# Handing the gate and up weights to TensorE in quarters of the contraction instead of halves

## The chip, the cores and the metric

The kernel runs on one core of a Trainium2 chip. The metric is the device time of one execution in microseconds, the median of several runs. The core has a matrix engine (TensorE, PE in the profile), VectorE (DVE), ScalarE (ACT), GpSimd (POOL) and SyncE (SP), which here only starts transfers. Sixteen DMA engines move data between the main memory (HBM) and the on-chip buffer (SBUF). They are shared by all queues; nearly all transfers of this kernel are started by SP and stand in its queue, q1.

## What is computed

One step of a decoder layer on 288 tokens of width 2048 (256 of a prompt, 32 of samples), in float32: a normed input projection, a convolution mixer and a pooling mixer, an output projection, and then a mixture of experts. Each token goes to two of 32 experts:

```python
for e in range(N_EXPERTS):
    a = jax.nn.silu(hf @ w_gate[e]) * (hf @ w_up[e])
    y = y + gates[:, e:e + 1] * (a @ w_down[e])
```

w_gate[e] and w_up[e] are 2048 x 512 (4 MB each), w_down[e] is 512 x 2048 (4 MB). So an expert costs 12.6 MB of weights, whatever the number of its tokens, and the 32 of them 403 MB. A final norm follows.

## The kernel before

The mixers and the output projection fill the first 372 us. Then come the routing and the experts. Tokens are sorted into blocks of 64 slots, one block for an expert, and the experts run in pairs (function `pair`, index i, with s = 0 and 1 for the even and the odd expert, n = 2i + s). For a pair, PE first gathers the tokens of the 128 slots with one-hot matrices (`select`, L694). For an expert it then runs the gate and up product (L716): 16 steps k of the contraction (2048 = 16 x 128), each with two matmuls of 512 columns, in four groups c of four steps. The profile counts every such float32 matmul twice, so a quarter c is 16 of its records. ScalarE and VectorE make silu(gate) times up, PE transposes the result (L731) and runs the down product (L737) in four steps q. VectorE and ScalarE scale the result, and POOL scatters the rows to a table in HBM (L1359, `expert_rows`). Five more pairs exist for experts with over 64 tokens; here they are skipped by branches.

**Buffers.** Gate and up weights of an expert lie in `wgu`, 64 KB of each partition; there is one such buffer, which every expert reuses. Only the first two steps k of an odd expert have a place of their own (`wgu_first`, loaded by `load_first`, L399). In HBM, each of the 128 partitions owns 16 consecutive rows k of w_gate (32 KB), so a transfer of half the contraction takes 16384 contiguous bytes for a partition. The down weights have two buffers (`wdn[0]`, `wdn[1]`), each filled in two halves h (`load_wd`, L407), again of 16384 bytes for a partition. Before the experts start, their first pieces are loaded by `load_wd_part` (L403) with 8192 bytes for a partition.

**Order of the transfers.** SP runs one program in order. `gate_up` waits until PE has counted `gu_used` up (once per quarter c, so 4 for an expert), then starts the gate and the up transfer of a half. `down` waits for `wd_used` in the same way. In steady state the queue holds, in this order: gate and up of an odd expert (without its first two steps), down of the next even one, its gate and up, the first two steps of the next odd one, its down, and so on. The last odd expert, 31, is written out: its down weights are started after its gate and up. PE waits for a landed half on `gu_in[0]` or `gu_in[1]` (L710).

**The end.** After its last weights have landed (L484) and the scatters are done (L487), SP starts six transfers (L491) that fetch the scattered rows of the three token tiles, two for each. VectorE adds the residual to the first of each tile (L1185). PE, which has stepped over the five skipped pairs, adds up the second part and the last expert's rows in PSUM (L788, L791), VectorE adds these (L1194), and a norm and the output transfers close the program. From the second tile on, L788 waits for L1194 of the tile before (`part_added`).

Of the kernel before, what the change touches and what calls it, by code (L numbers as in the profile page):

```python
# [105 lines left out]
def hybrid_decoder_step(nc, x_prompt, x_sample, state_conv, state_pool, g_mix, w_in, w_dw, b_dw, ln_g, ln_b,  # L106
# [3 lines left out]
    with ctx:  # L110
# [3 lines left out]
        def sem(name):  # L114
            return ctx.enter_context(nc.semaphore(name))
# [107 lines left out]
        wgu = words(arena, 0, GU_WORDS).rearrange("p (c g k f) -> p c g k f", c=2, g=2, k=8)  # L223
# [35 lines left out]
        half_in = sem("half_in")  # L259
        slot_in = [sem(f"slot_in{a}") for a in range(2)]  # L260
        first_in = sem("first_in")
        gu_in = [sem(f"gu_in{c}") for c in range(2)]
        wd_in = [[sem(f"wd_in{s}{h}") for h in range(2)] for s in range(2)]

        st_out = sem("st_out")
# [35 lines left out]
        gu_used = sem("gu_used")  # L301
# [68 lines left out]
        def _(sp):  # L370
# [18 lines left out]
            sp.dma_start(wsl[0][:, 0:CT, :], wpool).then_inc(slot_in[0], 16)  # L389

            def load_gu(e, c, g, s=0):
                k = 2 if s == 1 and c == 0 else 8 * c
                w = (wgate, wup)[g][:, bass.DynSlice(e, 1), k:8 * c + 8, :].rearrange("p o k f -> p (o k f)")
                sp.dma_start(wgu[:, c, g, k - 8 * c:8, :].rearrange("p k f -> p (k f)"), w).then_inc(gu_in[c], 16)  # L394

            def load_first(e):
                for g, src in ((0, wgate), (1, wup)):
# [12 lines left out]
            for c in range(8):  # L410
                if c == 0:
                    sp.wait_ge(u_mm, CT)
                elif c == 1:
                    sp.wait_ge(wp_mm, CT)
                else:
                    sp.wait_ge(o_mm, 2 * c - 2)
                sp.dma_start(wsl[(c + 1) % 2], wout[:, :, c * COL:(c + 1) * COL]).then_inc(slot_in[(c + 1) % 2], 16)
                if c == 1:
                    sp.wait_ge(st_out, 16 * 4)
                    sp.wait_ge(old_out, 16 * 2)  # L420
                if c in (1, 3, 4, 5):
                    load_gu(0, *((0, 0), (0, 1), (1, 0), (1, 1))[(1, 3, 4, 5).index(c)])
                if c == 6:
                    sp.wait_ge(mix_ready, CT)
                    load_wd_part(0, 0, 1, 1)
                    for a in range(2):
                        sp.wait_ge(x1_ready[a], CT // 2)
                    load_wd_part(1, 1, 0, 0)
# [10 lines left out]


            def gate_up(e, n, s):
                for c in range(2):
                    sp.wait_ge(gu_used, 4 * n + 2 * c - 2)
                    for g in range(2):
                        load_gu(e, c, g, s)

# [60 lines left out]
        def _(pe):  # L507
# [190 lines left out]
            def pair(i, first=False, ahead=True, last=False):  # L698

                for s in range(2):  # L700
                    n = 2 * i + s

                    for c in range(4):
                        if first and s == 0:
                            for b in ((0, 1), (2,), (3,), ())[c]:
                                select(0, b)
                        if s == 0:
                            pe.wait_ge(xgT_ready, 4 * i + c + 1)
                        if c % 2 == 0:
                            pe.wait_ge(gu_in[c // 2], 32 * n + 32)  # L710
                        if s == 1 and c == 0:
                            pe.wait_ge(first_in, 32 * i + 32)
                        for k in range(4 * c, 4 * c + 4):
                            w = wgu_first[:, :, k, :] if s == 1 and k < 2 else wgu[:, k // 8, :, k % 8, :]
                            for h in range(2):
                                mm = pe.matmul(ps[4 + s][BLK * h:BLK * (h + 1), :], xgT[:, k, BLK * s:BLK * (s + 1)],  # L716
                                                 w[:, :, 256 * h:256 * (h + 1)], start=(k == 0), stop=(k == KT - 1))
                        mm.then_inc(gu_used, 1)
# [701 lines left out]
```

## Time and profile before

| | us |
|---|---|
| median of 3 runs | 1390.73 |
| lowest to highest | 1390.59 to 1391.2 |
| the profiled execution, its own time | 1391.43 |
| span of the profiled execution | 1389.6 |
| PE busy | 1281.5 (92%) |
| DVE, ACT, POOL busy | 344.3, 101.4, 102.4 |
| granted TensorE clock, mean | 0.974 |
| moved by DMA | 464.61 MB, mean 334 GB/s |

The span is what the trace covers from its first to its last instruction. A busy PE is not PE at its peak, since the ends of matmuls are modelled. The DMA share is the part of the time in which the 16 engines worked on packets. A share over 1 means that packets of one engine overlap.

### The profile page before, as it was taken

How to read it: one execution, taken by the hardware profiler on the slowest of the kernel's cores; microseconds unless marked ns; L12 is line 12 of the kernel's file. 1: busy time of each engine (PE TensorE's matmuls, PEld its weight loads, DVE VectorE, ACT ScalarE, POOL GpSimd, SP SyncE). 2: the span in 40 equal slices, each digit the busy share in tenths (PEclk: the TensorE clock that was granted, in tenths of full speed). 3: DMA queues.
4: the chain of work that ended last, by engine and by line, in shares of the span. 5: the costliest groups of instructions: out<-in, count | busy, mean ns of one | idle time of the engine just before them, and what ended most of it. 6: DMA issues, size and time to landing. Idle time of an engine off the chain costs nothing.

```text
span 1389.6 us, 16405 instructions
## 1 busy us (share of the span) xinstructions
PE 1281.5 (92%) x6548; PEld 721.1 (52%) x6548; DVE 344.3 (25%) x699; ACT 101.4 (7%) x232; POOL 102.4 (7%) x164
## 2 busy tenths in 40 slices
PE   9999989999999998989998989899889989889876
PEld 7777767777865443444343445444344444334321
DVE  4499933011342110101101011110101101010226
ACT  2100012000100000000000000000000000000012
POOL 2211152000000000000000000000000000000000
PEclk9999999999999999999999999999999999999997
DMA  9444325565439999999999999999999999999894
GB/s 237 165 143 158 122 67 170 199 243 211 166 138 372 426 426 427 428 430 425 428 426 426 428 427 427 427 425 428 421 427 422 418 427 419 428 426 410 341 321 118
DMA packets 82486, 464.61 MB, mean 334 GB/s; under 512 B 8079, under 2 KB 50191, under 8 KB 56195
## 3 DMA queue, kind: packets, MB, share of 16 engines
q1 hardware_dynamic: 76784, 455.89, 81.3%
q0 software_dynamic: 5392, 7.86, 1.8%
q10 hardware_dynamic: 283, 0.48, 0.1%
q8 instruction: 19, 0.31, 0.1%
q14 instruction: 8, 0.07, 0.0%
HBM read 456.67 MB, written 20.80 MB: 344 GB/s over the span
## 4 chain that ended last, share of the span: by engine, by line
PE 44%; DMA 41%; issue 7%; DVE 5%; SPq 1%; ACT 0%; DVEq 0%; ACTq 0%
DMA arena<-in_w_up_dram 41%; PE bank L716 21%; PE bank L562 14%; PE bank L737 3%; DVE arena L979 3%; PE bank L694 2%; SPq L394 1%; PE bank L788 1%; PE bank L629 1%; PE bank L646 0%; PE bank L599 0%; PE bank L511 0%; PE bank L643 0%; PE bank L791 0%; DVE arena L985 0%
## 5 line engine op out<-in xcount | busy, mean ns | idle before, releaser
L716 PE MATMUL bank<-arena,stage 128*64 128x512 f32 x1920 | 442.8, 615 | 58.3 <-DMA arena<-in_w_up_dram 58.3
L716 PEld LDWEIGHTS bank<-arena,stage 128*64 128x64 f32 x1920 | 146.0, 142 | 347.6 <-issue 304.7
L562 PE MATMUL bank<-arena,stage 128*128 128x288 f32 x1280 | 315.0, 407 | 0.8 <-DVE arena L962 0.8
L562 PEld LDWEIGHTS bank<-arena,stage 128*128 128x128 f32 x1280 | 241.9, 190 | 66.3 <-issue 0.9
L694 PEld LDWEIGHTS bank<-x1w,x1r 96*128 96x128 f32 x1536 | 174.0, 192 | 26.0 <-issue 26.0
L694 PE MATMUL bank<-x1w,x1r 96*128 96x128 f32 x1536 | 180.2, 277 | 0.0
L1222 DVE TENSOR_TENSOR a_sb<-sl_sb,bank 128x256 f32<-128x256 f32 x32 | 19.3, 604 | 498.1 <-ACT sl_sb L895 498.1
L737 PE MATMUL bank<-arena,aT 128*64 128x512 f32 x512 | 113.4, 595 | 8.5 <-ACT aT L897 8.5
L979 DVE SCALAR_TENSOR_TENSOR arena<-arena,wdw 128x256 f32<-128x256 f32 x240 | 103.0, 503 | 0.0
L1359 POOL DMA_INDIRECT expert_rows<-ysb,cur_d x31 | 30.3, 978 | 855.9 <-DVE ysb L1236 827.8
L1236 DVE TENSOR_SCALAR ysb<-bank,wslot 128x512 f32<-128x512 f32 x31 | 23.3, 751 | 255.6 <-PE bank L737 255.6
L737 PEld LDWEIGHTS bank<-arena,aT 128*64 128x64 f32 x512 | 36.4, 137 | 75.3 <-issue 73.9
L737 PE MATMUL bank<-xT,aT 128*64 128x512 f32 x256 | 58.6, 598 | 7.4 <-ACT aT L897 7.4
L737 PE MATMUL bank<-stage,aT 128*64 128x512 f32 x256 | 57.8, 592 | 0.0
L1096 DVE TENSOR_TENSOR stage<-bank,gfp 128x512 f32<-128x512 f32 x64 | 42.5, 682 | 54.2 <-PE bank L694 54.2
L895 ACT ACTIVATE sl_sb<-bank 128x256 f32<-128x256 f32 x32 | 12.3, 383 | 484.9 <-PE bank L716 484.9
L908 ACT ACTIVATE ysb<-bank,wslot 128x512 f32<-128x512 f32 x31 | 21.3, 687 | 229.6 <-PE bank L737 219.2
L737 PEld LDWEIGHTS bank<-stage,aT 128*64 128x64 f32 x256 | 18.4, 137 | 36.6 <-issue 36.6
L737 PEld LDWEIGHTS bank<-xT,aT 128*64 128x64 f32 x256 | 16.9, 136 | 38.6 <-issue 27.4
L1017 DVE TENSOR_TENSOR x1w<-bank,xT 128x288 f32<-128x288 f32 x16 | 7.2, 453 | 93.7 <-PE bank L562 93.7
L716 PE MATMUL bank<-stage 128*64 128x512 f32 x128 | 30.3, 593 | 0.0
L511 PE MATMUL bank<-ones 128*128 128x128 f32 x186 | 26.3, 309 | 1.8 <-POOL ones L1275 1.8
(232 smaller groups left out, 483.8 us busy)
## 6 DMA issues: line engine op xcount, KB each, us to landing
arena<-in_w_gate_dram SPq DMA_DIRECT2D x48, 2048.0 KB, 13.7
arena<-in_w_up_dram SPq DMA_DIRECT2D x48, 2048.0 KB, 21.1
arena<-in_w_down_dram SPq DMA_DIRECT2D x30, 2048.0 KB, 17.9
xT<-in_w_down_dram SPq DMA_DIRECT2D x15, 2048.0 KB, 20.4
stage<-in_w_down_dram SPq DMA_DIRECT2D x15, 2048.0 KB, 21.7
arena<-in_w_gate_dram SPq DMA_DIRECT2D x16, 1536.0 KB, 14.8
arena<-in_w_up_dram SPq DMA_DIRECT2D x16, 1536.0 KB, 21.1
stage<-in_w_in_dram SPq DMA_DIRECT2D x11, 2048.0 KB, 8.2
```

Of the source, the lines that this page charges most:

```text
L394: sp.dma_start(wgu[:, c, g, k - 8 * c:8, :].rearrange("p k f -> p (k f)"), w).then_inc(gu_in[c], 16)
L511: pe.matmul(ps[bank][:, 0:P], ones[:, :], ones[:, :], start=True, stop=True)
L562: last = pe.matmul(ps[bank][:, 0:NTOK], wsl[a][:, k, cc * P:(cc + 1) * P], rhs[:, k, :], start=(n == 0), stop=(n == KT - 1))
L694: last = pe.matmul(ps[SELB[b]][:, (k % 4) * P:(k % 4 + 1) * P], x1r[:, t, k * P:(k + 1) * P], hot[:, t, :], start=(t == 0), stop=(t == TT ...
L716: mm = pe.matmul(ps[4 + s][BLK * h:BLK * (h + 1), :], xgT[:, k, BLK * s:BLK * (s + 1)], w[:, :, 256 * h:256 * (h + 1)], start=(k == 0), st ...
L737: mm = pe.matmul(ps[2 + m][BLK * h:BLK * (h + 1), :], aT[:, j * P + BLK * half:j * P + BLK * (half + 1)], wdn[s][half][:, j * D + 1024 * h ...
L908: act.activation(ysb[:, s, 0:512], ps[2][:, :], ACT.Copy, scale=dyn(wslot, n, 1)).then_inc(y0_ready, 1)
L979: ins = dve.scalar_tensor_tensor(out=(fin if w == W - 1 else dst), in0=src, scalar=wdw[:, cc, w:w + 1], in1=dst, op0=ALU.mult, op1=ALU.add)
L1096: dve.tensor_tensor(xgT[:, 4 * b:4 * b + 4, :], ps[SELB[b]][:, :].rearrange("p (k s) -> p k s", k=4), gfp[:, 4 * b:4 * b + 4, None].to_bro ...
L1222: dve.tensor_tensor(a_sb[:, :].rearrange("p (j f) -> p f j", j=2), sl_sb[:, :].rearrange("p (f j) -> p f j", j=2), ps[4 + s][:, 256:512].r ...
L1236: dve.tensor_scalar(ysb[:, s, 512:1024], ps[3][:, :], dyn(wslot, n, 1), None, ALU.mult).then_inc(y1_ready, 1)
L1359: pool.indirect_dma_start(out=yexp_dram, out_offset=bass.IndirectOffsetOnAxis(ap=at, axis=0), in_=rows, in_offset=None, bounds_check=4 * N ...
```

## The change

The gate and up weights of an expert are moved and released in quarters of the contraction. `load_gu` takes c from 0 to 3 and moves four steps k (8192 contiguous bytes for a partition) instead of eight; for an odd expert, c = 0 moves the two steps that `wgu_first` doesn't hold. `gu_in` has four semaphores, and PE waits for one ahead of every quarter. SP waits for `gu_used` ahead of each quarter, and for quarter c only until PE is done with the same quarter of the expert before: 4n + c - 3 in place of 4n - 2 and 4n for the two halves. An expert has eight such transfers instead of four. The first expert's weights, loaded during the output projection, are started in four places as before, now as gate and up of one quarter together rather than as one half of one matrix. Layout, bytes and arithmetic are the same.

```diff
@@ -259,7 +259,7 @@
         half_in = sem("half_in")
         slot_in = [sem(f"slot_in{a}") for a in range(2)]
         first_in = sem("first_in")
-        gu_in = [sem(f"gu_in{c}") for c in range(2)]
+        gu_in = [sem(f"gu_in{c}") for c in range(4)]
         wd_in = [[sem(f"wd_in{s}{h}") for h in range(2)] for s in range(2)]
 
         st_out = sem("st_out")
@@ -389,9 +389,10 @@
             sp.dma_start(wsl[0][:, 0:CT, :], wpool).then_inc(slot_in[0], 16)
 
             def load_gu(e, c, g, s=0):
-                k = 2 if s == 1 and c == 0 else 8 * c
-                w = (wgate, wup)[g][:, bass.DynSlice(e, 1), k:8 * c + 8, :].rearrange("p o k f -> p (o k f)")
-                sp.dma_start(wgu[:, c, g, k - 8 * c:8, :].rearrange("p k f -> p (k f)"), w).then_inc(gu_in[c], 16)
+                k0, k1 = (2 if s == 1 and c == 0 else 4 * c), 4 * c + 4
+                o = 8 * (c // 2)
+                w = (wgate, wup)[g][:, bass.DynSlice(e, 1), k0:k1, :].rearrange("p o k f -> p (o k f)")
+                sp.dma_start(wgu[:, c // 2, g, k0 - o:k1 - o, :].rearrange("p k f -> p (k f)"), w).then_inc(gu_in[c], 16)
 
             def load_first(e):
                 for g, src in ((0, wgate), (1, wup)):
@@ -419,7 +420,8 @@
                     sp.wait_ge(st_out, 16 * 4)
                     sp.wait_ge(old_out, 16 * 2)
                 if c in (1, 3, 4, 5):
-                    load_gu(0, *((0, 0), (0, 1), (1, 0), (1, 1))[(1, 3, 4, 5).index(c)])
+                    for g in range(2):
+                        load_gu(0, (1, 3, 4, 5).index(c), g)
                 if c == 6:
                     sp.wait_ge(mix_ready, CT)
                     load_wd_part(0, 0, 1, 1)
@@ -439,8 +441,8 @@
 
 
             def gate_up(e, n, s):
-                for c in range(2):
-                    sp.wait_ge(gu_used, 4 * n + 2 * c - 2)
+                for c in range(4):
+                    sp.wait_ge(gu_used, 4 * n + c - 3)
                     for g in range(2):
                         load_gu(e, c, g, s)
 
@@ -706,8 +708,7 @@
                                 select(0, b)
                         if s == 0:
                             pe.wait_ge(xgT_ready, 4 * i + c + 1)
-                        if c % 2 == 0:
-                            pe.wait_ge(gu_in[c // 2], 32 * n + 32)
+                        pe.wait_ge(gu_in[c], 32 * n + 32)
                         if s == 1 and c == 0:
                             pe.wait_ge(first_in, 32 * i + 32)
                         for k in range(4 * c, 4 * c + 4):
```

On SP, in the loop over pairs, this is the gate and up load of an even expert before (`wgu` lies in `arena`; 4096 elements are 16384 bytes):

```order
53 L394 DMA arena<-in_w_gate_dram 128x4096 [waits gu_used]
54 L394 DMA arena<-in_w_up_dram 128x4096
55 L394 ISA [waits gu_used]
56 L394 DMA arena<-in_w_gate_dram 128x4096
57 L394 DMA arena<-in_w_up_dram 128x4096
```

And the same place now (2048 elements are 8192 bytes; `L445` and `ISA` rows work out the number to wait for):

```order
65 L395 DMA arena<-in_w_gate_dram 128x2048 [waits gu_used]
66 L395 DMA arena<-in_w_up_dram 128x2048
67 L445 REGISTER_ALU
68 L395 ISA [waits gu_used]
69 L395 DMA arena<-in_w_gate_dram 128x2048
70 L395 DMA arena<-in_w_up_dram 128x2048
71 L445 REGISTER_ALU
72 L395 ISA [waits gu_used]
73 L395 DMA arena<-in_w_gate_dram 128x2048
74 L395 DMA arena<-in_w_up_dram 128x2048
75 L395 ISA [waits gu_used]
76 L395 DMA arena<-in_w_gate_dram 128x2048
77 L395 DMA arena<-in_w_up_dram 128x2048
```

Two waits and four transfers have become four waits and eight transfers.

On PE, in the loop, this is the gate and up product of the odd expert before (the first four matmuls read `wgu_first`, which lies in `stage`):

```order
211 L716 MATMUL bank<-stage 64x512 [waits first_in]
212 L716 MATMUL bank<-stage 64x512 x3
213 L716 MATMUL bank<-arena,stage 64x512 x12
214 L716 MATMUL bank<-arena,stage 64x512 [waits gu_in1]
215 L716 MATMUL bank<-arena,stage 64x512 x15
```

And now:

```order
215 L717 MATMUL bank<-stage 64x512 [waits first_in]
216 L717 MATMUL bank<-stage 64x512 x3
217 L717 MATMUL bank<-arena,stage 64x512 x4
218 L717 MATMUL bank<-arena,stage 64x512 [waits gu_in1]
219 L717 MATMUL bank<-arena,stage 64x512 x7
220 L717 MATMUL bank<-arena,stage 64x512 [waits gu_in2]
221 L717 MATMUL bank<-arena,stage 64x512 x7
222 L717 MATMUL bank<-arena,stage 64x512 [waits gu_in3]
223 L717 MATMUL bank<-arena,stage 64x512 x7
```

The one wait in the middle of the 32 matmuls has become three, one ahead of each further quarter; no matmul has moved.

## Rows read from the trace of the kernel before

**Rows 1.** The page: DMA share (tenths) and rate in 40 slices of the span.
```profile
DMA  9444325565439999999999999999999999999894
GB/s 237 165 143 158 122 67 170 199 243 211 166 138 372 426 426 427 428 430 425 428 426 426 428 427 427 427 425 428 421 427 422 418 427 419 428 426 410 341 321 118
```

**Rows 2.** Chain of waits, 560 to 640 us: start, duration, what the end hung on.
```profile
577.90 13.76 PE bank L716 x64
...
592.23 22.64 DMA arena<-in_w_up_dram
...
614.91 8.81 PE bank L716 x32
```

**Rows 3.** DMA queues in the saturated stretch, 540 to 1240 us: packets, MB, share.
```profile
DMA packets 26850, 297.99 MB, mean 426 GB/s; under 512 B 5104, under 2 KB 5104, under 8 KB 8891
...
q1 hardware_dynamic: 23538, 294.61, 99.4%
q0 software_dynamic: 3312, 3.39, 1.4%
```

**Rows 4.** DMA queue, 378 to 384.9 us: first halves of the down weights, 8192-byte rows.
```profile
DMA packets 407, 2.95 MB, mean 427 GB/s; under 512 B 47, under 2 KB 47, under 8 KB 47
...
q1 hardware_dynamic: 407, 2.95, 101.3%
```

**Rows 5.** DMA queue, 419 to 427 us: gate and up rows of 16384 bytes.
```profile
DMA packets 224, 3.41 MB, mean 426 GB/s; under 512 B 16, under 2 KB 16, under 8 KB 16
...
q1 hardware_dynamic: 224, 3.41, 99.6%
```

**Rows 6.** Timeline of SP and PE at the start of the expert stage.
```profile
396.83 3.65 PE L716 MATMUL bank<-arena,stage 128*64 128x512 f32 x16
...
407.13 0.34 SPq L394 DMA_DIRECT2D arena<-in_w_gate_dram  x1
...
432.90 1.94 PE L716 MATMUL bank<-stage 128*64 128x512 f32 x8
434.66 12.19 PE L716 MATMUL bank<-arena,stage 128*64 128x512 f32 x56
...
440.02 0.33 SPq L394 DMA_DIRECT2D arena<-in_w_gate_dram  x1
```

**Rows 7.** Windows: PE, PEld, DVE, ACT, POOL busy, clock, DMA share, GB/s.
```profile
440.00:441.00 1.00, 1.00 (x6) 0.29 (x4) 0.00 (x0) 0.00 (x0) 0.00 (x0) 1.00 0.39 119
...
1300.00:1305.00 5.00, 4.17 (x20) 1.15 (x16) 0.24 (x1) 0.00 (x0) 0.31 (x2) 1.00 0.48 197
...
1314.00:1315.00 1.00, 1.00 (x8) 0.49 (x6) 0.00 (x0) 0.00 (x0) 0.00 (x0) 1.00 0.14 61
1315.00:1316.00 1.00, 1.00 (x7) 0.19 (x3) 0.00 (x0) 0.02 (x1) 0.00 (x0) 1.00 0.17 74
```

**Rows 8.** Timeline of PE and SP, last two experts.
```profile
1304.21 0.33 SPq L394 DMA_DIRECT2D arena<-in_w_gate_dram  x1
...
1307.10 8.78 PE L716 MATMUL bank<-arena,stage 128*64 128x512 f32 x32 [2.93 <-DMA arena<-in_w_up_dram]
...
1315.91 0.33 SPq L394 DMA_DIRECT2D arena<-in_w_gate_dram  x1
...
1317.95 7.09 PE L737 MATMUL bank<-arena,aT 128*64 128x512 f32 x32 [0.46 <-ACT aT L897]
...
1326.58 12.19 PE L716 MATMUL bank<-arena,stage 128*64 128x512 f32 x56
...
1338.38 3.12 SPq L491 DMA_DIRECT2D arena<-expert_rows  x6
```

**Rows 9.** Timeline of DVE and PE in the last stage.
```profile
1358.21 3.68 DVE L1185 TENSOR_TENSOR arena<-arena,x1r 96x2048 f32<-96x2048 f32 x1 [3.19 <-DMA arena<-expert_rows]
1361.81 1.27 DVE L1194 TENSOR_TENSOR arena<-arena,bank 96x512 f32<-96x512 f32 x2
...
1364.89 1.96 PE L788 MATMUL bank<-arena,ident 96*96 96x512 f32 x4
```

## The prediction, made before the changed kernel ran

> **What bounds the kernel now.** I read the page's slices first. From slice 14, 450 us on, to slice 36 the DMA engines are full and move 420 to 430 GB/s; before that they have room [rows 1]. Such a stretch ends when its bytes are through. The chain of waits says the same from PE's side: PE does a half of the contraction, SP starts the next transfers, they land 22.64 us later, PE does the next half in 7 to 9 us and so on [rows 2]. A 2 MB transfer at 427 GB/s takes 4.9 us, so 22 us to landing is a queue of several transfers, not latency. PE has some 3 us to spare for an expert: it sat idle 2.93 us ahead of a half [rows 8]. So an earlier release or a finer wait can't speed up the middle. It counts only where the engines run dry, at the start and at the end; and whatever makes a byte dearer counts for all experts.
>
> **The price of smaller pieces.** Per expert and engine, 32 packets of 16384 bytes (or 12288) become 64 smaller ones, and four more transfers bring four more end packets of 4 bytes. The down weights at 378 us are already read in 8192-byte rows. There 407 packets, 360 of them of 8192 bytes and 47 ends, took 101.3% of 16 x 6.9 us, that is 111.8 us, or 0.621 us for two large ones with their ends [rows 4]. At 419 us, 208 packets of 16384 bytes and 16 ends took 99.6% of 16 x 8 us, 127.5 us, or 0.613 us each [rows 5]. The difference, 0.0084 us, times 32 is **0.27 us for an expert**. That is the dear end, since packets of one engine overlap: in the full stretch the shares of the two queues add up to 100.8%, and 0.8% of 16 x 700 us over 26850 packets is 3.3 ns for each [rows 3]. 36 new packets overlap their neighbours too, 0.12 us. I take **0.15 us**. The cheap end is nothing: the rates of the two stretches, 427 and 426 GB/s, don't differ [rows 4, 5]. Between the ends I stay with 0.15, as it is made of durations and their overlap, while the rates also hold the stretches' edges. Experts 2 to 31 come through the full queue: 30 x 0.15 = **+4.5 us** on the last landing, with 0 and 30 x 0.27 = 8.1 as ends.
>
> A rule speaks against the change here. The full queue shows no time between transfers: q1 alone is 99.4% busy with fourteen transfers for a pair of experts [rows 3]. The Trainium skill, page "DMA: Bandwidth & Descriptors", section "Anatomy of one DMA", gives a fit of a fixed 2.0 us for every transfer plus its bytes at 436 GB/s (for GpSimd's path), and "Rules for kernel authors" asks for at least 1 MiB per transfer for full bandwidth; the changed ones are just 1 MiB. If the 2 us stood in the stream, eight more transfers for a pair would make it 16 us longer, 240 us in all by that page; the trace doesn't agree that it does, since it is latency at the end of each transfer, behind which the next already moves.
>
> **Start of the expert stage.** Expert 2's first transfers wait for half of expert 1, which PE began at 432.90, and are started at 440.02. With the new wait, one quarter is enough: 432.90 + 3.6 = 436.5, with a quarter at 3.65 us [rows 6]. Before, the queue ran out: in 440 to 441 the engines were busy 0.39 of the time [rows 7], until the packets of 440.02 arrived some 1.2 us later. After, the new ones stand in the queue before it is empty. What counts is how long the engine that finished last was idle, not the mean over the engines. The last landing of an expert waits for the slowest, and some engines lag: in 1300 to 1305, with nothing started before 1304.21, 0.48 of them still worked [rows 7, 8]. I take **-0.7 us**, between 0.3 and the 1.4 us or so that the mean engine was idle. The releases before (407.13 comes forward by a quarter and a gather) fill room which the engines have anyway, since the stream is held up again by the down weights of expert 2, whose wait doesn't change.
>
> **End, transfers.** Expert 31's second half waits for all of expert 30 and starts at 1315.91. The queue had nearly run dry: 0.14 and 0.17 in the two microseconds before [rows 7, 8]. After, quarters 2 and 3 wait for quarters 2 and 3 of expert 30, and quarter 2 is queued before the first two are through. For the slowest engine this is **-0.6 us** (0 to 1.1). Sum for the landing of the last down weights, which now lets SP start L491 at 1338.38 [rows 8]: 4.5 - 0.7 - 0.6 = **+3.2 us**.
>
> **End, PE.** Expert 30's second half lands at about 1307.0, and PE then needs 8.78 us for 32 records before it goes on [rows 8]. After, only the last quarter is left, 3.65 us at full clock: the quarter before it landed 4.9 us earlier. That is **-5.1 us** (3.4 if PE runs at the lower clock again). The landing itself is 29 x 0.15 - 0.7 = 3.65 us later. PE's own chain through the down product of expert 30 (1317.95) and all of expert 31 [rows 8] so ends 3.65 - 5.1 = **-1.5 us**, earlier than before. Expert 31's last quarter (7 MB of gate and up and 1 MB of the first two steps, 19.6 us after the stream passes expert 30) is there before PE needs it, at some 23 us (3.65, then 2.05 to the down product, 7.09, and three quarters); its down weights are there within a microsecond of PE's need.
>
> **Which of the two ends last.** SP starts the six transfers of L491 only when the last down weights have landed. VectorE's third residual add waits for its rows until 1358.21; L1194 follows it at 1361.81, to 1363.08. PE's L788 for the second tile needs that and started at 1364.89, held by PE's own order [rows 9]. So the transfers have **1.8 us** of slack ahead of PE. The landing is 3.2 us late and PE is 1.5 us early, so the new last comer is the row transfers with VectorE's adds: the end moves by 3.2 - 1.8 = **+1.4 us**. From there the sequence of L788, L791, L1194 and the norm is unchanged.
>
> **Edits with one answer.** The extra waits of PE are in its own order and cost nothing while it has 3 us to spare for an expert. SP's four more starts for an expert, 0.33 us each, lie in its waits. Behind SP's new waits stand the down weights of the next expert; their turn in the queue comes over 10 us later, so nobody waits for that. Expert 0's weights are started in the output projection, where the engines have room [rows 1], and are long there. Should PE's spare time be gone, a wait would cost what it lasts; it would have to grow by 3 us for an expert first.
>
> **The rivals.**
> (a) The split costs its dear end. For: durations of packets are measured directly, the overlap is a mean. Against: 0.8% of overlap must be somewhere. Then the landing moves by 8.1 - 1.3 = +6.8 and the end by +5.0: **1395.7 us**, slower. It decides from 0.20 us for an expert, where 30 x 0.20 - 1.3 - 1.8 reaches 2.9 us. It ends on the other side.
> (b) The split costs nothing. For: equal rates [rows 4, 5]. Then the landing is 1.3 us early, PE is 0.7 + 5.1 = 5.8 us early, and the end is held by VectorE's first two L1194, 1.3 us earlier than 1363.08, against 1364.89: 3.1 us sooner, **1387.6 us**, faster.
> (c) Each start of a transfer leaves a hole. At 0.1 us for each of 120 new transfers, +12 us: about **1401 us**, slower. Against: fourteen transfers for a pair leave no visible hole in 700 us [rows 3]. This is the page's rule in a mild form.
>
> **How the numbers follow.** The sum is made on the profiled execution (span 1389.6, own time 1391.43), which lies 0.7 us above the median, so the change is added to the median 1390.73: **1392.1 us**. About 0.2%, 2.8 us, is what a measurement can tell from none. The forecast with its variants (0.03 to 0.19 us for an expert) has 0.52, (a) 0.27, (b) 0.15, (c) 0.06. So: within 0.2% 0.52, slower 0.33, faster 0.15. The range leaves out most of (c), the dear tail of (a) and the cheapest of (b): 1388.0 to 1397.0. The forecast's own range is 1389 to 1393.5.
>
> **What the changed profile would show.** The step on price: the time from one landing of the last gate and up transfer to the next, over many experts, grows by 0.15 us from about 30 (12.7 MB with the scatter at 426 GB/s [rows 3]); 0.27 or 0 would speak for (a) or (b). Packets of about 0.310 us for 8192 bytes, the DMA share still 1.01 and no dip between transfers; a dip speaks for (c). The step on the start: no slice under 0.9 between 436 and 442 us. The step on the end: 16 records of L717 after the last wait of expert 30 instead of 32, the down product of expert 31 ending 1 to 2 us before 1348, while SP starts the row transfers near 1341.5 instead of 1338.38, and VectorE's last residual add starts near 1361.4. The forecast is wrong if rows in the middle are dearer than at 378 us, where few other packets ran, if the slow engines' lag changes, or if the row transfers themselves take another time at their new place.

## The result, and the profile after

The changed kernel took 1402.89 us in the median of 20 runs (1393.76 to 1409.87), the kernel before 1390.38 us in 20 (1388.87 to 1392.86). The ratio is 1.0084, 95% interval 1.0061 to 1.0108: slower, and above the whole range that was forecast (1388 to 1397). The middle of its ten faster runs, 1395.0, would lie inside that range. The spread is as telling as the median. The 20 times of before lie within 4 us. Those of the changed kernel fall into two groups: ten from 1393.76 to 1398.83 us (middle 1395.0) and ten from 1406.96 to 1409.87 us (middle 1408.3), with nothing between. So there are two things to explain: +4.6 us in the lower group, and 13 us more in the upper one.

The profile of one execution of the lower group (1394.51 us). Page: busy time, DMA share and rate in 40 slices, and the gate and up product (busy, mean ns, idle before it):

```profile
span 1392.7 us, 16789 instructions
...
PE 1266.9 (91%) x6548; PEld 713.5 (51%) x6548; DVE 343.8 (25%) x699; ACT 101.5 (7%) x232; POOL 102.4 (7%) x164
...
DMA  9444325565449999999999999999999999999974
GB/s 239 163 148 153 121 71 168 200 245 204 174 182 367 421 423 425 423 423 422 423 423 424 422 423 422 422 423 424 422 423 422 422 421 423 421 422 420 372 270 128
...
L717 PE MATMUL bank<-arena,stage 128*64 128x512 f32 x1920 | 429.4, 595 | 74.4 <-DMA arena<-in_w_up_dram 74.4
```

Against [rows 1] most of the full slices move 422 to 424 GB/s instead of 425 to 428. The DMA engines are as full as before, with more packets for the same bytes. From 540 to 1240 us:

```profile
DMA packets 40074, 295.87 MB, mean 423 GB/s; under 512 B 6573, under 2 KB 6573, under 8 KB 13132
...
q1 hardware_dynamic: 36762, 292.48, 99.9%
q0 software_dynamic: 3312, 3.39, 1.4%
```

40074 packets for 295.87 MB, where [rows 3] had 26850 for 297.99 MB; the shares of the queues add up to 101.3% instead of 100.8%. So the packets overlap more in sum, as assumed, but their durations have grown by more than that gives back. For the 12.58 MB of an expert, q1's packets took 0.994 x 700 us / 294.61 MB x 12.58 MB = 29.71 us of every engine before, and 0.999 x 700 / 292.48 x 12.58 = 30.08 us now: +0.37 us.

How much this costs an expert is best read from the chain of waits, from landing to landing of the last gate and up transfer of an expert. The kernel before (start, duration, what it was):

```profile
531.85 22.66 DMA arena<-in_w_up_dram
...
1284.39 22.57 DMA arena<-in_w_up_dram
```

The changed kernel:

```profile
527.25 26.27 DMA arena<-in_w_up_dram
553.57 3.68 PE bank L717 x16
557.82 26.00 DMA arena<-in_w_up_dram
583.95 3.67 PE bank L717 x16
...
1287.07 26.14 DMA arena<-in_w_up_dram
1313.35 3.67 PE bank L717 x16
```

Before: 554.51 to 1306.96 us for 25 experts, **30.10 us** each. After: 553.52 to 1313.21, **30.39 us**. The transfers now need 26 us instead of 22.6 from start to landing (they are started a quarter earlier), and PE does 16 records after the last one, 3.68 us, where [rows 2] had 32 in 7 to 9 us. None of that shortens the period.

The end of the same execution: timelines of PE, then of SP, then of VectorE.

```profile
1308.42 3.65 PE L717 MATMUL bank<-arena,stage 128*64 128x512 f32 x16 [1.56 <-DMA arena<-in_w_up_dram]
1313.35 3.65 PE L717 MATMUL bank<-arena,stage 128*64 128x512 f32 x16 [1.28 <-DMA arena<-in_w_up_dram]
...
1347.12 1.89 PE L738 MATMUL bank<-stage,aT 128*64 128x512 f32 x8
1356.27 3.70 PE L789 MATMUL bank<-arena,ident 96*96 96x512 f32 x4 [7.27 <-issue]
...
1368.01 1.93 PE L789 MATMUL bank<-arena,ident 96*96 96x512 f32 x4 [2.61 <-DVE arena L1195]
...
1343.55 3.94 SPq L493 DMA_DIRECT2D arena<-expert_rows  x6
...
1362.98 3.69 DVE L1186 TENSOR_TENSOR arena<-arena,x1r 96x2048 f32<-96x2048 f32 x1 [2.77 <-DMA arena<-expert_rows]
1366.58 2.47 DVE L1195 TENSOR_TENSOR arena<-arena,bank 96x512 f32<-96x512 f32 x4
```

This is the end that was forecast, step by step. PE's last wait for expert 30 is followed by 16 records instead of the 32 of [rows 8]. SP starts the row transfers at 1343.55 instead of 1338.38. VectorE's third residual add starts at 1362.98 instead of 1358.21 [rows 9], and PE, which had come last before, now stands 2.61 us in front of L789 (L788 before) for VectorE's L1195. It starts the second tile at 1368.01 instead of 1364.89, +3.1 us, and that is the whole difference of the two spans (1392.7 and 1389.6).

### The profile page after: what moved, and what is told of

It reads as the page before. It is cut to its first block, busy times and chain, and to the rows that moved or that the text cites. A ratio compares the mean times of both kernels' runs of the same rounds, so it can differ in the third digit from the quotient of the medians.

```text
span 1392.7 us, 16789 instructions
## 1 busy us (share of the span) xinstructions
PE 1266.9 (91%) x6548; PEld 713.5 (51%) x6548; DVE 343.8 (25%) x699; ACT 101.5 (7%) x232; POOL 102.4 (7%) x164
## 4 chain that ended last, share of the span: by engine, by line
DMA 52%; PE 33%; issue 7%; DVE 5%; SPq 1%; ACT 0%; DVEq 0%; ACTq 0%
DMA arena<-in_w_up_dram 49%; PE bank L564 13%; PE bank L717 12%; DVE arena L980 3%; PE bank L696 2%; PE bank L738 2%; DMA stage<-in_w_down_dram 2%; DMA arena<-expert_rows 1%; SPq L395 1%; PE bank L631 1%; PE bank L648 0%; PE bank L601 0%; PE bank L645 0%; DVE arena L986 0%; DVE arena L1195 0%
## 5 line engine op out<-in xcount | busy, mean ns | idle before, releaser
L717 PE MATMUL bank<-arena,stage 128*64 128x512 f32 x1920 | 429.4, 595 | 74.4 <-DMA arena<-in_w_up_dram 74.4
L717 PEld LDWEIGHTS bank<-arena,stage 128*64 128x64 f32 x1920 | 139.4, 137 | 356.9 <-issue 293.4
L1360 POOL DMA_INDIRECT expert_rows<-ysb,cur_d x31 | 30.3, 978 | 858.6 <-DVE ysb L1237 832.1
L717 PE MATMUL bank<-stage 128*64 128x512 f32 x128 | 30.3, 593 | 0.0
```

The lines of the kernel that those rows point to most:

```text
L1360: pool.indirect_dma_start(out=yexp_dram, out_offset=bass.IndirectOffsetOnAxis(ap=at, axis=0), in_=rows, in_offset=None, bounds_check=4 * N ...
```

## The experiments

Each ran beside the kernel before on the same chip. A time is the median of its runs; "group" means the two groups above. Half of the changed kernel's runs are of the upper one, so five runs that show none of it would come by chance once in 32.

**1. The changed kernel again**, without an edit.

> The changed kernel once more, for more times and a second trace. Its 20 times fall in two groups, 1394 to 1399 us and 1407 to 1410 us, while the trace with 1394.5 us shows 30.39 us from landing to landing of the last gate and up transfer of successive experts (before: 30.10). Theory P (packets and transfer ends make the stream dearer, and on some runs on one DMA engine more than on the others): in a run of the slow group the period is about 30.8 us, the middle takes all of the additional 13 us and the end looks the same. Rival E (something at the start or the end goes one of two ways, such as a transfer that misses its turn): the period stays 30.39 in both groups, and the 13 us show in one place.

Six times: 1398.13 twice, and 1406.75 to 1409.28 four times. The profiled one is of the upper group (1409.28 us). Its last landing, and its end (SP, then PE):

```profile
1289.07 26.18 DMA arena<-in_w_up_dram
```

```profile
1345.61 3.37 SPq L493 DMA_DIRECT2D arena<-expert_rows  x6
...
1349.14 1.89 PE L738 MATMUL bank<-stage,aT 128*64 128x512 f32 x8
1373.49 3.70 PE L789 MATMUL bank<-arena,ident 96*96 96x512 f32 x4 [22.46 <-issue]
```

The last landing is at 1315.25, the period over 25 experts (from 555.39) 30.39 us, as in the other trace. The landing is 2.0 us later than in the other trace, and the row transfers and PE with it. The rest of the difference of 14.8 us between the two spans stands in one row: PE ended its last down product at 1351.0 and then stood **22.46 us** before the first L789, where the lower group's trace has 7.27: 15.2 us more, less the 2.6 us of standing for VectorE that fall away. "issue" says that it waited for nothing the profile shows. In between it steps over the five skipped pairs, each a jump over a large piece of program. What else differs there is PE's code. Queue q8 carries instructions, 16 KB a packet; the profile doesn't name the engine, and that it is PE's is read from when its packets come. The two views, 1335 to 1375 us, of the lower group's trace and of this one:

```profile
q8 instruction: 3, 0.05, 0.6%
```

```profile
q8 instruction: 5, 0.08, 1.1%
```

Three packets of code against five. So rival E of this run held: the middle is the same in both groups.

**2. Split in halves.** The transfers of the changed kernel, the waits of before.

```diff
-                k = 2 if s == 1 and c == 0 else 8 * c
-                w = (wgate, wup)[g][:, bass.DynSlice(e, 1), k:8 * c + 8, :].rearrange("p o k f -> p (o k f)")
-                sp.dma_start(wgu[:, c, g, k - 8 * c:8, :].rearrange("p k f -> p (k f)"), w).then_inc(gu_in[c], 16)
+                for a, b in ((2 if s == 1 and c == 0 else 0, 4), (4, 8)):
+                    w = (wgate, wup)[g][:, bass.DynSlice(e, 1), 8 * c + a:8 * c + b, :].rearrange("p o k f -> p (o k f)")
+                    sp.dma_start(wgu[:, c, g, a:b, :].rearrange("p k f -> p (k f)"), w).then_inc(gu_in[c], 16)
...
-                            pe.wait_ge(gu_in[c // 2], 32 * n + 32)
+                            pe.wait_ge(gu_in[c // 2], 64 * n + 64)
```

> Eight transfers of 8192 bytes for a partition as in the changed kernel, but released and waited for in halves as before. Theory P: as dear in the middle as the changed kernel (30.4 us or more for an expert), and without the gains at the start and at the end: 1397 to 1400 us in the faster group, 1410 to 1414 in the slower, if it has one. Rival H (the finer hand-over itself disturbs the stream, by transfers started at other moments): 30.1 us for an expert and the time of the kernel before, about 1391 us.

1399.71 us (1397.69 to 1401.07), ratio 1.0064 (1.0051 to 1.0077), one group. Period 30.39 us, last landing of expert 30 at 1315.91. The whole dearer stream is there without the finer hand-over; what the hand-over gives is missing (some 4.7 us against the lower group), and so is the upper group. Theory P's first half held.

**3. Pieces of 8192 bytes in transfers of 2 MB.** The buffer is laid out by quarters (c=4, k=4), and a half of a matrix is one transfer with two pieces for each partition. The cut shows the main lines; the first half of an odd expert is left out, two transfers for each matrix.

```diff
+                    sp.dma_start(wgu[:, 2 * c:2 * c + 2, g, :, :].rearrange("p b k f -> p b (k f)"),
+                                 src.rearrange("p o (b k) f -> p (o b) (k f)", b=2)).then_inc(gu_in[c], 16)
```

> Four transfers of 2 MB for an expert as before, in halves, but the buffer is laid out by quarters, so that each partition's row is written in two pieces of 8192 bytes (an odd expert's first half is two transfers for each matrix). The number of pieces is that of the changed kernel, the number of transfers nearly that of before. If the pieces cost (32 more for an expert and DMA engine, at about 5 ns): 30.3 us for an expert, 1395 to 1398 us. If the transfers cost (their starts or their ends): near 1391 to 1392 us.

1400.62 us (1399.68 to 1402.09), ratio 1.0070 (1.0057 to 1.0083); period 30.38 us, where 30.3 us and 1395 to 1398 us were expected: at 5 ns for a piece the price was put too low. The pieces cost, not the number of transfers: this kernel has ten of them for a pair of experts instead of sixteen and pays the same.

**4. Pieces of 4096 bytes**, four transfers for an expert. The cut leaves out the buffer's layout.

```diff
+                w = (wgate, wup)[g][:, bass.DynSlice(e, 1), k:8 * c + 8, :].rearrange("p o (b k) f -> p (o b) (k f)", k=2)
+                sp.dma_start(wgu[:, 4 * c + (k - 8 * c) // 2:4 * c + 4, g, :, :].rearrange("p b k f -> p b (k f)"), w).then_inc(gu_in[c], 16)
```

> Four transfers for an expert in halves, each partition's row written in pieces of 4096 bytes: 128 pieces for an expert and DMA engine instead of 32. The pieces of 8192 bytes cost 0.29 us for an expert by the landings (30.39 against 30.10 us), that is 9 ns for each of the 32 additional ones. If each piece costs the same: 96 additional ones, +0.87 us, 30.97 us for an expert, and 1417 to 1419 us. If the price comes from something of 8192 bytes only, or from the layout, 30.4 us and 1400.

1412.27 us (1411.78 to 1415.48), ratio 1.0159 (1.0144 to 1.0173). From the chain, the first and the last landing:

```profile
537.56 19.91 DMA arena<-in_w_up_dram
...
1306.54 23.19 DMA arena<-in_w_up_dram
```

557.47 to 1329.73 us is 30.89 us for an expert, +0.79. The 96 additional pieces of the expectation hold for an even expert only; an odd one had pieces of 4096 and 12288 bytes before and gets 80. Between the two landings q1 has 60692 packets, and 25287 in the kernel before between its own two, which makes 88 more for an expert and DMA engine. That is 9.0 ns for each, next to 8.7 ns for each of 32 in rows_8k (+0.28) and 9 ns in the changed kernel (+0.29, with four more transfer ends). The price goes with the number of pieces. The whole time came out 5 us under the 1417 expected, 2 of them by the pieces that aren't there.

**5. Eight transfers over half the partitions**, with pieces of 16384 bytes.

```diff
+                for p0 in (0, 64):
+                    w = (wgate, wup)[g][p0:p0 + 64, bass.DynSlice(e, 1), k:8 * c + 8, :].rearrange("p o k f -> p (o k f)")
+                    sp.dma_start(wgu[p0:p0 + 64, c, g, k - 8 * c:8, :].rearrange("p k f -> p (k f)"), w).then_inc(gu_in[c], 16)
```

> Eight transfers for an expert of 1 MB, each with 64 partitions and rows of 16384 bytes (12288 for an odd expert's first half), in halves. The number of transfers is that of the changed kernel, the pieces are those of before. If the transfers cost: as much as the changed kernel without its gains, 1396 us or more, with two groups if these come from transfers. If the pieces cost: 1391 to 1392 us, one group.

2137.76 us (1970.56 to 2165.64). It was meant to count transfers and instead showed something else. DMA queues, 600 to 1200 us:

```profile
DMA packets 13540, 143.47 MB, mean 239 GB/s; under 512 B 3110, under 2 KB 3110, under 8 KB 4830
...
q1 hardware_dynamic: 11956, 141.66, 93.8%
```

The engines were 93.8% busy and moved 239 GB/s: for the same bytes, q1's packets took 1.7 times as long, on the mean over this stretch (0.938 x 600 us for 141.66 MB, against [rows 3]). All six runs show it; why is open. It can't tell transfers from pieces; experiment 3 did.

**6. PE's extra waits alone.** The kernel before, with PE waiting ahead of every quarter for the landed half.

```diff
-                        if c % 2 == 0:
-                            pe.wait_ge(gu_in[c // 2], 32 * n + 32)
+                        pe.wait_ge(gu_in[c // 2], 32 * n + 32)
```

> The kernel before; only PE waits ahead of every quarter, twice for the same landed half, so that its program has the rows of the changed kernel while no transfer changes. In the trace of the slower group (1409.28 us) PE stood still for 22.5 us between the last down product and the first L789, while it stepped over the five skipped pairs, against 7.3 us in the trace of 1394.5 us and 7.9 in the kernel before. Theory C (it is PE's own program: the waits have changed where its code is fetched): two groups, 1391 and about 1405 us. Rival T (it is the moment at which PE comes there, or what the transfers do then): one group at 1390 to 1392 us.

1390.65 us (1389.32 to 1392.87), 11 runs, ratio 0.9996 (0.9987 to 1.0005), one group. The waits are free, and PE's longer program alone does not make the upper group.

**7. and 8. One branch around the skipped pairs**, in the changed kernel and in the one before.

```diff
+            with pe.If(n_over > 0):
-            with pe.Fori(0, OVP) as j:
+                with pe.Fori(0, OVP) as j:
```

> The changed kernel with one more branch on PE, around the loop over the five skipped pairs, so that PE jumps once instead of five times. If the stepping over is the slower group's 13 us: one group at about 1394 to 1395 us (the faster group keeps its time, since VectorE and the row transfers end last there, not PE). If the slower group has another cause, two groups stay.

> The kernel before with the same one branch. There PE ends last (L788 of the second tile started 1.8 us after VectorE had made it possible). If the 7.9 us of stepping over shrink to some 2 us, the end moves to VectorE's order, 1.8 us sooner: 1388.6 us. If jumping once costs as much, 1390.5.

The changed kernel with it: 1399.40 us (1397.12 to 1400.44), one group, ratio 1.0057 (1.0044 to 1.0070). The upper group is gone, but the time is not that of the lower one, 1394 to 1395, that was expected. PE came to the first L790 (L788 before) 3 us sooner, had to stand for VectorE longer, 4.98 us, and ran the next matmuls at half its clock:

```profile
1353.47 3.70 PE L790 MATMUL bank<-arena,ident 96*96 96x512 f32 x4 [3.98 <-DMA arena<-expert_rows]
...
1367.61 3.70 PE L790 MATMUL bank<-arena,ident 96*96 96x512 f32 x4 [4.98 <-DVE arena L1196]
```

3.70 us where the changed kernel had 1.93 for the same four; with the four behind them the trace loses 2.7 us by that. The kernel before with one branch: 1389.53 us (1385.44 to 1392.15, 12 runs), ratio 0.9989 (0.9980 to 0.9999), some 1.2 us better: the only version here whose interval lies below 1, and only just. PE stands 4.03 us, where the kernel before had 7.91, and VectorE ends last:

```profile
1352.93 3.70 PE L789 MATMUL bank<-arena,ident 96*96 96x512 f32 x4 [4.03 <-issue]
...
1364.05 1.93 PE L789 MATMUL bank<-arena,ident 96*96 96x512 f32 x4 [2.16 <-DVE arena L1195]
```

**9. Quarters for the last two experts only.** Experts 0 to 29 keep their halves. The cut leaves out `load_quarter` and PE's waits for quarters in the last pair.

```diff
+            def gate_up_quarters(e, s):
+                for c in range(4):
+                    sp.wait_ge(gu_used, 4 * e + c - 3)
+                    for g in range(2):
+                        load_quarter(e, c, g, s)
...
+            next_weights(NE - 3, last=True)
+            gate_up_quarters(NE - 1, 1)
```

> The kernel before, in which only experts 30 and 31 are loaded, released and waited for in quarters; the other 30 keep their halves and rows of 16384 bytes. So the stream stays at 30.1 us for an expert. By the terms of the sum that held in the trace of 1394.5 us (last quarter instead of last half: PE 5.1 us earlier; down weights of expert 31 landing 0.6 us earlier or so; VectorE's order in between), the end is 2 us earlier: 1388 to 1389 us. Theory M (the slower group comes from the moment at which PE steps over the skipped pairs, now about 5 us after SP has started the row transfers, in the kernel before 9.5 us): a second group at about 1402 us. Rival X (it comes from the eight transfers in the middle): one group.

Twelve times in two groups again: six from 1387.72 to 1393.07 us and six from 1401.03 to 1403.31 (median of all 1397.05, ratio 1.0035, 1.0010 to 1.0059). Its trace is one of the upper group (1402.00 us): PE, then SP, then the code queue, 1335 to 1375 us.

```profile
1343.10 1.89 PE L756 MATMUL bank<-stage,aT 128*64 128x512 f32 x8
1366.88 3.70 PE L807 MATMUL bank<-arena,ident 96*96 96x512 f32 x4 [21.90 <-issue]
...
1339.62 3.33 SPq L508 DMA_DIRECT2D arena<-expert_rows  x6
...
q8 instruction: 5, 0.08, 1.1%
```

21.90 us of standing, five packets of code. So the upper group needs nothing of the middle; the hand-over in quarters at the end is enough for it. The lower six have their middle at 1390.7 us, next to 1391.43 for the kernel before, and not the 1388 to 1389 expected: PE's last product ended 2.9 us sooner (1345.0 instead of 1347.9), but the row transfers, which wait for the last down weights, started at 1339.62, 1.2 us later than the 1338.38 of before and not 0.6 sooner. Why these landed later is open.

**10. The same with one branch.**

> The same with one branch around the skipped pairs on PE. One group without the 13 us, at 1388 to 1390 us. It would be the kernel that beats both; PE may idle so long that its clock is low in the first L789 of the second tile (3.70 instead of 1.93 us in after_one_branch), which would cost 2 us of it.

1393.38 us (1390.30 to 1395.35, 11 runs), ratio 1.0015 (1.0006 to 1.0024): one group, and worse than the kernel before, where 1388 to 1390 were expected. The row transfers started at 1340.74, and the first matmuls of the second tile took 3.70 us at the low clock, after 6.35 us of standing for VectorE.

**11. The kernel before, row transfers later.** SP waits for half of expert 31's down product too.

```diff
             sp.wait_ge(zero_out, 16)
+            sp.wait_ge(last_down, 1)
```

> The kernel before; only SP waits, ahead of the row transfers L491, also for the first half of expert 31's down product, so that they start at about 1344.7 instead of 1338.4 us, 3.4 us before PE begins to step over the skipped pairs. All weights move as before. VectorE's third add comes 6.3 us later, less the slack of 1.8: 1395 us. Theory M: a second group some 10 us above. Rival X: one group at 1395.

1398.89 us (1397.05 to 1400.36), one group. The row transfers started at 1344.23, 3.2 us before PE was done; a late start of them alone doesn't make the upper group. It costs 7.5 us against the 1391.43 beside it instead of the 4.5 expected (6.3 less the slack of 1.8). PE stood 6.19 us for VectorE and then took 3.70 and 1.86 us for eight matmuls that took 1.96 and 1.10 before: 2.5 us of the 3.0 more.

**12. The changed kernel, PE later.** 16 idle matmuls ahead of the stepping over.

```diff
+            stay_awake(16, 4)
             with pe.Fori(0, OVP) as j:
```

> The changed kernel; only PE does 16 idle matmuls (5 us) between the last down product and the stepping over, so that it steps 10 us after the row transfers' start, as in the kernel before. Theory M: one group, at 1396 to 1398 us (PE's first L789 5 us later than in the trace of 1394.5 us, where 2.6 us were slack). Rival X: two groups, 1397 and 1412.

1399.73 us (1399.40 to 1401.10), one group, five runs within 1.7 us.

```profile
1350.62 3.84 PE L513 MATMUL bank<-ones 128*128 128x128 f32 x32
1364.98 3.70 PE L790 MATMUL bank<-arena,ident 96*96 96x512 f32 x4 [10.53 <-issue]
```

From the idle matmuls' end at 1354.5, 9.1 us after the row transfers' start, it takes 10.5 us to L790. Theory M held in this: when PE comes 3.8 us later, the upper group is gone. The time is above the 1396 to 1398 expected, since the stepping over took 10.5 us and not 7.3.

**13. and 14. Row transfers later, in the changed kernel and in last_two** (the edit of 11).

> The changed kernel; only SP waits, ahead of the row transfers, also for the first half of expert 31's down product, so that they start at about 1345.6 instead of 1343.6 us. Theory F (PE's code, fetched by the same DMA engines once it is some 1 to 3 us into that product, waits behind the row transfers when these have just started): the fetch is through before them, one group at 1396 to 1397 us, PE's stepping over in 7 us or less. Rival M2 (only PE's own moment counts, such as where its program stands when the last weights land): two groups as before, 1396 and 1409.

> The same wait in the kernel that has quarters for experts 30 and 31 alone; the row transfers start at about 1341.4 instead of 1339.6 us. Theory F: one group at 1391 to 1394 us. Rival M2: two groups, 1392 and 1402.

The changed kernel with it: 1401.63 us (1401.02 to 1404.11), one group, PE 6.38 us from its last product to the first L790 (the row transfers end that wait), three packets of code. The group is gone, but the time is 5 us above what was expected: the row transfers started at 1346.77 instead of 1345.6, and the low clock took the rest (L790 3.70 us after 6.55 of standing). last_two with it: six times from 1393.76 to 1401.19 us, spread, neither one tight group nor the two of before; its trace (1393.92 us) has three packets. 1391 to 1394 us were expected; the trace is of its second fastest run and says nothing of the slower ones. Theory F is supported by the first and not settled by the second.

## Why the prediction was wrong, point by point

**What bounds the kernel: right.** The middle is the stream's, and PE's finer waits and releases change nothing in it (experiments 2 and 6 against the changed kernel).

**The price of smaller pieces: the term that was mis-sized, by two.** The sum took 0.15 us for an expert; it is 0.29. 29 experts make that 4 us more than the forecast had on expert 30's last landing. The step that failed is the duration of a packet, read at 378 us, where it ran with little beside it: that gave 0.27 us for an expert, and in the full stream it is 0.37, by the rows of q1 in 540 to 1240 us. The same sum over the 25 experts of split_in_halves and rows_8k gives 0.42 and 0.38 us. Of this the period shows 0.28 to 0.29; some 0.1 us is given back by packets that overlap, and the prediction had put that at 0.12. So its deduction for overlap was sound, and its warning about rows in the middle being dearer than at 378 us named what went wrong.

Rival (a) has 0.27 us and 1395.7, close to the 0.29 and to the middle of the lower group, 1395.0. That is luck in part. It denies an overlap that is there, and its packets are too cheap by about as much; its time leans on gains at the start and the end that came out larger (below). The time of rival (c) was also added up wrongly: 12 - 1.3 - 1.8 is +8.9, 1399.6 us and not 1401.

That the number of transfers is free was right: rows_8k with ten for a pair of experts has 30.38 us, the changed kernel with sixteen 30.39. By the fit of a fixed 2.0 us for a transfer in the Trainium skill, "DMA: Bandwidth & Descriptors", section "Anatomy of one DMA" (made for GpSimd's path), six transfers would be 12 us for a pair, an estimate from that page, if this time stood in the stream; the traces don't agree that it does.

**The start: right in kind, too small by 1.2 us.** Where the engines were busy 0.45 and 0.39 of the time in the two microseconds from 439 us on before, they now are 0.97 and 0.94. Two slices between 436 and 442 us still lie under the 0.9 that was forecast, 0.86 in the first and 0.66:

```profile
437.00:438.00 1.00, 1.00 (x8) 0.36 (x6) 0.00 (x0) 0.00 (x0) 0.00 (x0) 1.00 1.19 250
438.00:439.00 1.00, 1.00 (x6) 0.29 (x4) 0.00 (x0) 0.00 (x0) 0.00 (x0) 1.00 0.66 262
439.00:440.00 1.00, 1.00 (x8) 0.35 (x6) 0.00 (x0) 0.00 (x0) 0.00 (x0) 1.00 0.97 365
440.00:441.00 1.00, 1.00 (x8) 0.36 (x6) 0.00 (x0) 0.00 (x0) 0.00 (x0) 1.00 0.94 377
```

Last landings of expert 30 were 1306.96, 1307.53, 1308.04 and 1308.23 us in four traces with the old stream, and 1313.21, 1315.25, 1313.56, 1314.59 and 1314.20 in five of the changed one: 6.5 us apart in the mean. 29 x 0.29 is 8.4, so the start gave back about 1.9 us, not 0.7, and more than the 1.4 that the prediction had as its most. split_in_halves, with the old start, lands at 1315.91, the full 8.2 us after them. Single traces of one kernel differ by 1 to 2 us, so more than "about 2" can't be said.

**The end: right in its order, and it decided the lower group.** 5.1 us were forecast for PE, and the slack of 1.8 us, and that VectorE with the row transfers becomes the new last comer; the rows show each. The gain of the transfers at the end was put at 0.6 us, between 0 and 1.1. From the last gate and up landing of expert 30 to the row transfers it was 31.42 us before and is 30.34 and 30.36 in the two traces of the changed kernel, with one expert in between that costs 0.29 more: 1.4 us gained. The row transfers came 5.2 us late instead of 3.2. With these sizes the sum reads 8.7 - 1.9 - 1.4 - 1.8 = +3.6, and 3.1 is what the trace has; the middle of the lower group lies 4.6 above the median of before. With the price alone put right it would have read 8.7 - 0.7 - 0.6 - 1.8 = +5.6; that the forecast's +1.4 came within 2 us of the trace is luck, since the two gains were put too low as well.

**The upper group: a step that was missing, and the one that took the median out of the range.** The prediction said "From there the sequence of L788, L791, L1194 and the norm is unchanged" and took PE's 7.91 us of "issue" ahead of L788 for a constant. It isn't one. It is PE stepping over five large pieces of program, whose code comes as packets of queue q8, in the same stretch as the row transfers. The Trainium skill, "DMA: Bandwidth & Descriptors", section "Issuing engines are not separate DMA queues", says that transfers started by ScalarE, SyncE and GpSimd run on the same 16 DMA engines and interleave. The trace agrees for SP's and GpSimd's queues ([rows 3]: 99.4% and 1.4% of the 16 engines), and q8 stands in the same list, with 0.6% or 1.1%. What the runs show:
- in both traces of an upper group it takes 22 us with five packets of code between 1335 and 1375 us; in the thirteen others (all but experiment 5) PE's first matmul of the last stage comes 4 to 11 us after its last product or idle matmuls, with two or three packets, and in five of these it is the row transfers that end the wait, so the stepping itself was shorter;
- it needs the end in quarters (changed kernel, last_two), not the dearer stream (2, 3, 4: one group) nor the extra waits (6);
- it goes away when PE comes 3.8 us later (12), when PE jumps once (7, 10), and, in the changed kernel, when the row transfers start some 2 us later against PE (13).

In the kernel before, PE arrives 9.5 us after SP has started the row transfers; in the changed kernel and in last_two it is 5.4, in both groups of the former. What does differ between the two groups is when the code comes. Cutting the view of the queues at single microseconds, the lower group's trace has its first packet of q8 between 1344 and 1345 us, 1 us after the row transfers' start at 1343.55 and 4.5 us before PE ends its last product. In the upper group's trace the first comes between 1353 and 1354 us, 8 us after the row transfers' start at 1345.61 and 2.5 us after PE has ended, and five have come by the first L789. Over all twelve traces with the five separate branches, one or two packets have come before PE ends its last product in ten, which stepped over in 11 us or less, and none in two, which took 22. With one branch, two of three traces have none by then either (7, 10), and PE stood 4 us: one packet came before its next matmul, not five.

So the code came behind the row transfers in the slow case and ahead of them in the fast one, as theory F has it. In the traces of the changed kernel, of last_two and of experiments 7 and 12, the row transfers start 1.6 to 2.1 us after PE has begun its last down product, and the first packet of code falls on either side of them (2.6 us in 10, where it came behind). With 3.9 and 4.3 us (13) it came first, in one trace each. In the kernel before, the rows start 2.4 us ahead of that product, and the code, 8 us behind them, still comes 1.5 us before PE ends. This is read from single traces, and no run moved the code alone. Which side a run falls on stays open, and so does the spread of last_two_late_rows.

## What to carry to other kernels

Where a queue is full for most of a kernel, each piece has a price that adds up over all of it, while a finer hand-over earns only at the two ends. To cut the pieces there alone is the obvious next step, and it is not shown to pay: neither version of it here beat the kernel before (9, 10). Read a price from the stretch in which it will be paid; the price that packets showed in a quiet one was a quarter too low (0.27 us for 0.37). A stretch marked "issue" on the last engine's path is work with a cause of its own; before it is called unchanged, ask what it does and which shared resource it needs.

## What the runs showed of the hardware that was not expected

- A transfer over 64 of the 128 partitions with rows of 16384 bytes runs the stream at 239 GB/s instead of 426, with the engines as busy (experiment 5).
- An additional piece costs some 9 ns of every DMA engine's time in a full stream, at 4096 as at 8192 bytes: 0.28 us for 32, 0.79 us for 88.
- PE's way over the skipped program of five pairs took 6 to 11 us in ten traces and 22 us in two, in the same kernel from run to run; in the two, no packet of its code had come before it ended its last product.
- With two stops of 1.3 to 1.9 us for an expert TensorE stayed at its full clock of 2.4 GHz (16 records in 3.65 us, twice), where one stop of 2.9 us was in some experts followed by a stretch at 1.2 GHz (8.78 us for 32, [rows 8], and 7.1 in the others): the granted clock over the span rose from 0.974 to 0.991. In a kernel bound by its transfers that bought nothing. Stops of 5.0 to 6.6 us at the end did cost: 3.70 instead of 1.93 us for four matmuls (experiments 7, 10, 11, 13), where stops of 2.2 and 2.6 us did not (8, and the lower group).
